# A triangular solve on TensorE: products of 64 moving columns split into two halves of 64 stationary columns

## What is computed

```python
def wkv7_scan(r, w, k, v, a, b):
    '''S_t = S_{t-1} diag(w_t) + (S_{t-1} a_t) b_t^T + v_t k_t^T ;  y_t = S_t r_t.'''
    def step(state, inp):
        r_t, w_t, k_t, v_t, a_t, b_t = inp
        sa = jnp.einsum('bhvk,bhk->bhv', state, a_t)
        state = (state * w_t[:, :, None, :] + sa[..., None] * b_t[:, :, None, :]
                 + v_t[..., None] * k_t[:, :, None, :])
        return state, jnp.einsum('bhvk,bhk->bhv', state, r_t)
...
```

## Time and profile before

| | |
|---|---|
| median of three runs | 2134.86 us (2129.15 to 2138.71) |
| the profiled execution | 2133.44 us |
| span of its trace | 2131.6 us |
| TensorE busy | 2009.1 us (94%) |
| VectorE, ScalarE, GpSimd busy | 1182.1, 1144.7, 762.8 us |
| granted TensorE clock, mean | 0.959 of full |
| the solve (L992) in the trace | 418.7 to 636.7 us |

### The profile page before, as it was taken

How to read it: one execution, slowest core, us unless ns; L and a number is a source line. 1 busy time by engine, 2 the same in 40 slices (tenths; PEclk the granted TensorE clock), 3 DMA queues, 4 the chain that set the end, 5 groups by cost and what they waited for, 6 DMA issues and landing times.

```text
span 2131.6 us, 30022 instructions
## 1 busy us (share of the span) xinstructions
PE 2009.1 (94%) x11504; PEld 1740.8 (82%) x11504; DVE 1182.1 (55%) x1694; ACT 1144.7 (54%) x1538; POOL 762.8 (36%) x316
## 2 busy tenths in 40 slices
PE   6999999999999999989989999999979789999997
PEld 6998978888997789979867788888868578888885
DVE  2223655745445132236121788888844558888886
ACT  4344555333336344343354577777754347777775
POOL 6887765500008778868755000000037110000000
PEclk9999989999999999989999899999989789999999
DMA  6555433300004455535436698889634159889882
GB/s 228 180 194 178 140 119 138 119 1 2 1 12 162 145 191 188 186 138 178 177 133 236 243 346 332 337 335 348 268 126 171 54 226 343 339 335 349 340 338 107
DMA packets 59271, 425.47 MB, mean 200 GB/s; under 512 B 6545, under 2 KB 7057, under 8 KB 8081
## 3 DMA queue, kind: packets, MB, share of 16 engines
q1 hardware_dynamic: 57024, 415.26, 52.5%
q10 hardware_dynamic: 2128, 8.58, 1.1%
HBM read 422.76 MB, written 1.05 MB: 199 GB/s over the span
## 4 chain that ended last, share of the span: by engine, by line
PE 90%; DVE 6%; ACT 2%; issue 1%; DMA 1%; POOL 0%; ACTq 0%; DVEq 0%; POOLq 0%
PE ps L679 21%; PE ps L705 19%; PE ps L1230 10%; PE ps L992 9%; PE ps L1189 7%; PE ps L1191 7%; PE ps L1190 7%; PE ps L1177 2%; PE ps L1244 2%; PE ps L1212 1%; PE ps L726 1%; PE ps L862 1%; DMA par<-in_params 1%; DVE arena L2129 1%; PE ps L770 1%
## 5 line engine op out<-in xcount | busy, mean ns | idle before, releaser
L649 POOL TENSOR_TENSOR w_low<-ring,w_high 128x1024 fp32r<-128x1024 f32 x312 | 762.6, 2450 | 949.0 <-ACT w_high L1327 948.4
L1327 ACT ACTIVATE w_high<-ring 128x1024 fp32r<-128x1024 f32 x480 | 504.6, 1060 | 517.0 <-PE ps L705 233.4
L2293 DVE TENSOR_TENSOR w_low<-arena,w_high 128x1024 fp32r<-128x1024 f32 x312 | 373.7, 1222 | 52.0 <-ACT w_high L1327 48.7
L679 PE MATMUL ps<-x_high,w_high 128*128 128x256 f32 (+1 forms) x1288 | 372.3, 290 | 11.4 <-DVE x_low L1795 10.2
L679 PE MATMUL ps<-x_low,w_high 128*128 128x256 f32 (+1 forms) x1288 | 366.1, 286 | 0.0
L679 PE MATMUL ps<-x_high,w_low 128*128 128x256 f32 (+1 forms) x1288 | 365.9, 285 | 0.0
L1327 ACT ACTIVATE w_high<-arena 128x1024 fp32r<-128x1024 f32 x312 | 323.6, 1059 | 70.2 <-PE ps L1191 53.4
L679 PEld LDWEIGHTS ps<-x_high,w_high 128*128 128x128 f32 (+1 forms) x1288 | 249.5, 195 | 17.3 <-issue 7.9
L1189 PE MATMUL ps<-w_high,x_high 128*128 128x512 f32 x640 | 257.8, 403 | 2.8 <-DVE x_low L2375 2.8
L679 PEld LDWEIGHTS ps<-x_low,w_high 128*128 128x128 f32 (+1 forms) x1288 | 249.7, 195 | 2.9 <-issue 2.2
L1191 PE MATMUL ps<-w_high,x_low 128*128 128x512 f32 x640 | 250.9, 392 | 0.0
(11 more groups left out here) (293 smaller groups left out, 2406.6 us busy)
## 6 DMA issues: line engine op xcount, KB each, us to landing
ring<-in_stream SPq DMA_DIRECT2D x240, 1024.0 KB, 4.8
arena<-in_stream SPq DMA_DIRECT2D x156, 1024.0 KB, 4.9
arena<-in_gains ACTq DMA_DIRECT2D x4, 512.0 KB, 3.7
con<-in_consts ACTq DMA_DIRECT2D x1, 1280.0 KB, 7.3
con<-in_consts ACTq DMA_DIRECT2D x1, 1216.0 KB, 15.1
x<-in_x ACTq DMA_DIRECT2D x1, 1024.0 KB, 10.5
arena<-in_gate_bias ACTq DMA_DIRECT2D x1, 1024.0 KB, 5.7
out_dram<-arena ACTq DMA_DIRECT2D x1, 1024.0 KB, 4.1
```

Source lines behind the costliest of these rows:

```text
L649: nc.gpsimd.tensor_tensor(w_low[:, t % AHEAD, :], slot(SLOT[t // 2])[:, t % 2 * TW:t % 2 * TW + TW], w_high[:, t % AHEAD, :].bitcast(F32), ...
L679: mm = pe.matmul(dst, wp[rows, t % AHEAD, w], xp[rows, x0 + k, :], start=(k == 0 and n == 0), stop=(k == k_tiles - 1 and n == 2))
L1327: nc.scalar.activation(w_high[:, t % AHEAD, :], slot(SLOT[c])[:, t % 2 * TW:t % 2 * TW + TW], ACT.Copy)\
L2293: nc.vector.tensor_tensor(w_low[:, t % AHEAD, :], slot(SLOT[c])[:, t % 2 * TW:t % 2 * TW + TW], w_high[:, t % AHEAD, :].bitcast(F32), ALU. ...
```

## The change

A helper `halves` takes the place of `mm` for the 256 products of 64 moving columns and 128 stationary ones. It makes two products: the first with stationary columns 0-63 into PSUM partitions 0-63, the second with stationary columns 64-127 into partitions 64-127. The moving operand is the same for both. The last of them raises the lane's semaphore.

```diff
+                def halves(out_, lhsT, rhs, start=True, stop=True):
+                    for at in (0, 64):
+                        last = mm(out_[at:at + 64, :], lhsT[:, at:at + 64], rhs, start, stop)
+                    return last
...
                             elif st == 2:
                                 mm(a[:, 0:P], dd, dT)
                                 mm(a[:, P:2 * P], dT, dd)
-                                last = mm(a[:, 256:320], mbk[i][:, 256:384], Vtok[:, c, hc], stop=(c == 0))
+                                last = halves(a[:, 256:320], mbk[i][:, 256:384], Vtok[:, c, hc], stop=(c == 0))
                                 if c:
-                                    last = mm(a[:, 256:320], AR[rows, 2 * p + c, 0, :], state[rows, p, :], start=False)
+                                    last = halves(a[:, 256:320], AR[rows, 2 * p + c, 0, :], state[rows, p, :], start=False)
...
                             elif st == 6:
-                                last = mm(b[:, 0:64], tT, Wl[i])
+                                last = halves(b[:, 0:64], tT, Wl[i])
                             elif st == 7:
-                                last = mm(b[:, 0:64], nT, Ul[i])
+                                last = halves(b[:, 0:64], nT, Ul[i])
                             elif st == 8:
                                 mm(a[:, 0:P], n2, n2T)
-                                last = mm(b[:, 0:64], n2T, Ul[i])
+                                last = halves(b[:, 0:64], n2T, Ul[i])
                             elif st == 9:
-                                last = mm(b[:, 0:64], N4T[i], Ul[i])
+                                last = halves(b[:, 0:64], N4T[i], Ul[i])
                             else:
                                 if c:
-                                    mm(a[:, 0:64], AR[rows, 2 * p + c, 1, :], state[rows, p, :], stop=False)
-                                mm(a[:, 0:64], mbk[i][:, 128:256], Ul[i], start=(c == 0), stop=False)
-                                last = mm(a[:, 0:64], mbk[i][:, 384:512], Vtok[:, c, hc], start=False)
+                                    halves(a[:, 0:64], AR[rows, 2 * p + c, 1, :], state[rows, p, :], stop=False)
+                                halves(a[:, 0:64], mbk[i][:, 128:256], Ul[i], start=(c == 0), stop=False)
+                                last = halves(a[:, 0:64], mbk[i][:, 384:512], Vtok[:, c, hc], start=False)
```

## The result

The changed kernel takes 2140.11 us (median of 12 runs, 2131.39 to 2143.16) against 2133.54 us for the kernel before (median of 12, 2124.59 to 2138.71). The ratio is 1.0034, with a 95% interval of 1.0023 to 1.0046: 6 to 7 us slower. The forecast of +7 us was set on a median of 2134.86.

The account below looks back on a forecast made before the run. TensorE, busy 94% of the span, was taken to bound the kernel, by loading 128 stationary columns twice. Width changes less savings gave +9 us, the clock -2: +7 on the 2134.86 us median, 2142 us; range 2133 to 2171.

Parts of the forecast that it names:

- The forecast case: Whole kernel: the two column halves run at once, +9 - 2 = +7 us, 2142 us; chance 0.58.
- Cost of a change of width: TensorE in the solve: any change of the array's split costs 0.14 us, 0.21 to 0.22 if 128 columns move.
- Steps 6 and 7: Solve steps with three products a lane: from 0.67 us to 0.91 with halves at once, +0.24 a lane.
- step 8: Solve step with two products a lane: from 0.45 us to 0.69 with halves at once, +0.24 a lane.
- Halves at once: Every split product: both column halves run together, as row halves in step 1; a pair costs 0.116 us, before 0.223.
- The other rule: Rival for the split products: halves run one after the other, +33.6 us, 2168.5 us; chance 0.29.
- Step 10, chunk 0: Solve step where all records become narrow: from 0.96 us a lane to 0.46 with halves at once, -0.50.
- The wait between steps 9 and 10: TensorE, done early with step 9, waits for VectorE's add before step 10: 0.15 us a group.
- Step 10, chunk 1: Solve step with products over 64 partitions: from 0.95 us a lane to 0.63 with halves at once, -0.32.
- Step 2: Solve step where TensorE waits for VectorE's masks: extra cost hidden but for the last lane, +0.24 us in chunk 0.
- The clock: Two falls to 1.2 GHz in step 10 of chunk 1, together 4.6 us, may vanish; half taken back, -2 us.
- The sum: Solve with halves at once: +0.9 us a group of chunk 0, +1.4 of chunk 1, four each: +9.1 us.

## Why the prediction was right

The forecast case, both halves at once, is what the chip does, and the total, +6.6 us by the medians, is near the forecast +7. That it is so near is in part luck, as the last point says. Point by point:

- **Cost of a change of width**, 0.14 us or a little more where 128 columns move: right. Steps 6 and 7 were put at 0.91 us and took 0.91; step 8 at 0.69, took 0.68. The last full-width record to the first narrow one took 0.21 (464.28 to 464.49), not 0.22.
- **Halves at once**: right. The row halves of step 1 were the right nearest case, although column halves share their rows. The rule of the Trainium skill (TensorEngine Tiling (Array Packing), Key Properties) that tiles load and multiply in parallel holds here for fp32 products and for columns. The other rule that the prediction weighed, in the Trainium skill (TensorE: Matmul & The Clock Gate, Part 3: Packing small matmuls), that a load overlaps with running products only where the row group differs, doesn't hold here by its letter: the two halves have the same rows, and their products, each behind its own load, started within 0.01 us of each other at 464.49.
- **Step 10, chunk 0**: 0.46 us put, 0.37 found. The old narrow products alternate between column halves from lane to lane, so that over two lanes each column half gets the same number of records. Four lanes were put 0.4 us too dear.
- **The wait between steps 9 and 10**: 0.15 us put. The rows of TensorE in very short windows show the last record of step 9 and the first of step 10, 0.34 us apart, of which 0.06 is the record itself:

```profile
474.03 0.22 PE L992 MATMUL ps<-arena 128*64 128x64 f32 x1
474.37 0.28 PE L992 MATMUL ps<-arena 128*64 128x64 f32 x2
```

  So 0.28 us, 0.13 too cheap. Together with the last point, a group of chunk 0 came out at +0.67, put at +0.9.
- **Step 10, chunk 1**: 0.63 put, 0.64 found; the group +1.38, put at +1.4.
- **Step 2**: hidden but for the last lane, 0.24 us. Right (25.72 against 25.49 with step 2 whole).
- **The clock**: the direction in chunk 1 was right. Both falls in step 10 are gone in all three profiles, and group 6 went from 28.84 to 27.01 us in spite of its 1.4 us more. I took back 2 of these 4.6 us, against new falls elsewhere. Those came: two in step 2, 1.7 and 1.5 us, in two profiles out of three, though one such fall was seen in the kernel before as well.
- **The sum**: the terms as they are printed give +0.86 and +1.34 us a group, 8.8 in eight; the 9.1 of the prediction is a matter of rounding. Measured it is 8.2 (four groups of +0.67 and four of +1.38).
- **What wasn't in the sum**: the collision of VectorE with GpSimd behind the solve, 4.0 us. The first profiles add up so: 3.1 us earlier up to the first full group, +5.7 in the solve, +6.4 behind it, together +9.0. Of these the 3.1 are there before the solve's first product (418.7 and 415.5 us; in the fourteen profiles it lies between 410.4 and 419.5), where the program is the same. Of the 6.4, 2.4 come long after the collision. The stretch behind the solve took 1494.6, 1497.7 and 1494.6 us in the profiles of before and 1501.0, 1498.4 and 1498.4 in those of the changed kernel, so these 2.4 are no more than the scatter of one kernel. The closeness of 6.6 to 7 owes something to terms that cancel: the changes themselves (8.2 us), the new falls and the price behind the solve, less the falls that vanished (4.6). The mechanism of the forecast is shown; the last us of agreement are not.

## What to carry to other kernels

Splitting a product into column halves gains where many of its kind stand together, and loses where it stands between products of another shape: on this trace a change of the array's split and back costs 0.28 us at least, and a pair of halves saves 0.11. Count the changes in the order of the instructions before you count the products, and gather the products of one shape over independent lanes first; so the halves of steps 6 to 8 went from some +23 us to a gain of about 3. When a stage changes, look at the stage behind it as well: there the meeting of VectorE with GpSimd cost 4 us, half of what the change itself cost in the solve (8.2).

## What the hardware showed unexpectedly

- All four quarters of the array ran at once: four fp32 records of 64 rows and 64 columns, all under way within 0.29 us, from two lanes.
- Two streams of half-width records kept up their pace of 0.058 us each: twelve records in about 0.37 us, one in 0.031. The prediction had feared a limit on how fast they are issued; none was seen down to there.
- VectorE's four operations of 128x512 on fp32 data in SBUF went from 4.9 to 10.2 us beside GpSimd's `tensor_tensor`, when that had no pause. The last two took 1.3 us together in GpSimd's pause, and 5.6 without it.
